# Block stack on one core: experts' front by token tile, norm factor moved, time mix with keys first

## What is computed

```
n   = rmsnorm(h, norm2_g)
q   = (n @ w_q) in 8 heads of 2 x 128
s1, s2 = q[:128] @ keys1.T, q[128:] @ keys2.T        (128 scores each)
16 best of s1, 16 best of s2, 16 best of their 256 sums -> idx (of 16384 experts), ts
g   = softmax(ts)
act = gelu(sum_d u[idx] * n)
out = sum_k (g * act)_k * v[idx]_k
```

## Time and profile before

| | us |
|---|---|
| runs shown (3) | 1532.51, 1533.3, 1535.24; median 1533.3 |
| the profiled execution, its own time | 1537.3 |
| its span in the trace | 1535.5 |
| PE, DVE, ACT, POOL busy | 1353.6, 819.4, 406.3, 293.1 |
| first gather issued | 866.96 |
| last dot begins | 1522.87 |
| mean granted clock of PE | 0.976 |

### The profile page before, as it was taken

How to read it: one execution, slowest core, us unless ns; L and a number is a source line. 1 busy time by engine, 2 the same in 40 slices (tenths; PEclk the granted TensorE clock), 3 DMA queues, 4 the chain that set the end, 5 groups by cost and what they waited for, 6 DMA issues and landing times. The chain is left out here.

```text
span 1535.5 us, 18607 instructions
## 1 busy us (share of the span) xinstructions
PE 1353.6 (88%) x7074; PEld 884.5 (58%) x7074; DVE 819.4 (53%) x1944; ACT 406.3 (26%) x955; POOL 293.1 (19%) x269
## 2 busy tenths in 40 slices
PE   5999999989999899999999799998777777777776
PEld 3445799978577786888888645443323333333322
DVE  6305567425633143422211767777777777777654
ACT  3003312111152115355101322222222232222212
POOL 0000000000000010000000244446443444444430
PEclk8999999999999999999999999999999999999999
DMA  7443100044322424532244599999999999999994
GB/s 264 137 151 127 53 3 3 1 156 132 124 91 87 139 76 136 173 110 83 89 154 150 211 421 421 421 421 423 420 421 422 420 422 421 421 422 421 421 421 197
DMA packets 65108, 367.97 MB, mean 240 GB/s; under 512 B 7229, under 2 KB 8637, under 8 KB 31933
## 3 DMA queue, kind: packets, MB, share of 16 engines
q0 software_dynamic: 37152, 269.50, 42.3%
q1 hardware_dynamic: 27870, 97.30, 18.7%
HBM read 365.72 MB, written 1.05 MB: 239 GB/s over the span
## 5 line engine op out<-in xcount | busy, mean ns | idle before, releaser
L2056 PE MATMUL bank<-arena 128*128 128x512 f32 x580 | 273.4, 616 | 75.0 <-ACT arena L2130 74.9
L1475 PE MATMUL bank<-arena,ring 128*128 128x256 f32 (+1 forms) x1136 | 254.9, 385 | 7.1 <-DVE arena L1738 3.1
L2282 POOL DMA_INDIRECT arena<-peer_in,arena x145 | 162.3, 1119 | 499.2 <-DVE arena L2199 311.9
L2056 PEld LDWEIGHTS bank<-arena 128*128 128x128 f32 x580 | 108.0, 194 | 232.3 <-issue 231.8
L1475 PEld LDWEIGHTS bank<-arena,ring 128*128 128x128 f32 x1136 | 215.6, 191 | 41.2 <-issue 3.5
L2249 DVE CUSTOM_DVE_ANT_0 arena<-arena 128x1024 f32<-128x1024 f32 x145 | 176.9, 1225 | 74.6 <-DMA arena<-peer_in,arena 74.4
L2130 ACT ACTIVATE arena<-cst,arena 128x128 f32<-128x128 f32 x256 | 88.8, 394 | 139.9 <-DVE arena L2212 139.9
L442 PE MATMUL bank<-ring,arena 128*128 128x512 f32 x256 | 112.5, 602 | 0.0
L2056 PE MATMUL bank<-ring,arena 128*128 128x512 f32 x176 | 86.5, 632 | 26.2 <-ACT arena L2130 26.2
L2123 ACT ACTIVATE arena<-arena 128x2 f32<-128x2 f32 x128 | 26.0, 203 | 304.1 <-DVE arena L2249 304.0
L442 PEld LDWEIGHTS bank<-ring,arena 128*128 128x128 f32 x256 | 49.4, 193 | 62.1 <-issue 62.1
(11 more groups left out here) (349 smaller groups left out, 1832.0 us busy)
## 6 DMA issues: line engine op xcount, KB each, us to landing
ring<-stream_in SPq DMA_DIRECT2D x162, 512.0 KB, 3.3
ring<-stream_in SPq DMA_DIRECT2D x8, 384.0 KB, 5.0
arena<-peer_in,arena POOLq DMA_INDIRECT x145, 34.5
row<-rows_in SPq DMA_DIRECT2D x4, 512.0 KB, 18.3
cst<-cst_in SPq DMA_DIRECT2D x1, 1929.0 KB, 18.1
res<-res_in SPq DMA_DIRECT2D x2, 544.0 KB, 4.3
row<-rows_in POOLq DMA_DIRECT2D x2, 512.0 KB, 4.8
cst<-rg_w_in SPq DMA_DIRECT2D x1, 1024.0 KB, 7.1
```

Of the source, the lines that this page charges most:

```text
L1475: mm = nc.tensor.matmul(bank[:, first:first + width], slot[:, at + k * cols:at + (k + 1) * cols], src[:, k, :], start=k == 0, stop=k == kt ...
L2056: mm = nc.tensor.matmul(core.banks[2 * t + b][:, :], diag[i % ND], value_half(i, b), start=first, stop=last)
L2282: pool.indirect_dma_start(out=places[seat[i]], out_offset=None, in_=g.names["peer"], in_offset=bass.IndirectOffsetOnAxis(ap=index[:, i:i + ...
```

## The change

1. **Time mix.** The stream has the key slots first and the LoRA slot behind them. DVE makes the mixture k first, then w, a, v, r, g. PE projects k first, waiting for two column blocks of the mixture at a slot, then does LoRA and z, then v, r, g. ACT copies the keys first.
2. **Mixing projection.** In the second mix PE does the eight panels for tile 0 alone (128 columns). DVE adds each to x and multiplies the sum by the norm's gain (`g.n2`, without the norm's factor). ACT's squares go. The ring keeps the eight slots; tile 1's panels (`mix_second`) are done in the experts' stage, four to a bank.
3. **First queries.** Queries 0 and 1 leave the ring: their weights come to a place of their own (`first_wq`), issued behind the last mixing slot. They are computed tile by tile.
4. **The norm's factor.** Ones-matmul, root, reciprocal and scaling in front of the queries go. Scores and dots are made from the unnormed n2. ACT's `root(t)` squares the turned x row by row with a sum, and takes the root; DVE inverts it to `rstd[:, t]` (one number for each token). The exponential takes `chosen - max` times it, the Gelu the dot times it.
5. **Order in the experts' stage.** On PE: first queries of tile 0, scores(0), turns of n2 and x for tile 0, `mix_second`, first queries of tile 1, turns of x and n2 for tile 1, queries 2 and 3, scores(1), then the pairs; queries 4 and 5 and scores(2) stand behind the first three pairs. DVE routes unit 0, adds tile 1's banks, scales n2's tile 1, and takes the first dots; it routes unit 1 in one piece behind the third pair, and unit 2 by five steps behind each pair from the fifth on.
6. **Places.** 9 at first; 3 (res, first_wq, the mixing input) when x of tile 1 has been turned; 5 from gather 72 on.

```diff
 def weight_slots():
-    out = [("lora", 2 * KT * LORA)]
+    out = []
     for name in ("k", "v", "r", "g"):
         out += [((name, half, kp), SLOT) for half in range(2) for kp in range(KT // 2)]
+        if name == "k":
+            out += [("lora", 2 * KT * LORA)]
...
-    out += [(("wq", m), SLOT) for m in range(2 * HP)]
+    out += [(("wq", m), SLOT) for m in range(FIRST, 2 * HP)]
...
@@ time mix, PE
+            def project(n, name):
+                if n:
+                    pe.wait_ge(mixed.handle, 3 * KT + n)
...
+                        if not n and not half:
+                            pe.wait_ge(mixed.handle, 2 * kp + 2)
...
+            project(0, "k")
             slot = core.weights(pe, "lora")
...
@@ time mix, DVE
-            for name, n in (("w", 1), ("a", 4), ("k", 2), ("v", 3), ("r", 0), ("g", 5)):
+            for name, n in (("k", 2), ("w", 1), ("a", 4), ("v", 3), ("r", 0), ("g", 5)):
...
@@ time mix, SP
-            core.load_weights(sp, g.stream, 1)
+            core.load_weights(sp, g.stream, RING)
             sp.dma_start(lora2[0:LORA + 1, :], g.low2_in).then_inc(*g.lora_loaded.dma())
-            core.load_weights(sp, g.stream, RING)
...
@@ second mix, PE
-                panel("mix", m, tiles(Y, T), KT, T).then_inc(*full(("mix", m)))
-                core.used_by(("mix", m), ("mix", m))
+                bank = claim(pe, ("mix", 0, m))
+                panel("mix", m, tiles(Y, T)[:, :, 0:P], KT, P, bank=bank).then_inc(*full(("mix", 0, m)))
...
@@ second mix, ACT
-            for m in range(KT):
-                copied(act, ("mix", m))
-                nc.scalar.activation(g.squares_d[:, m, :], x[:, m, :], ACT.Square).then_inc(*g.squared_d.up())
...
@@ second mix, DVE
-                nc.vector.tensor_tensor(x[:, m, :], x[:, m, :], bank[:, 0:T], ALU.add).then_inc(*free(key))
+                nc.vector.tensor_tensor(x[:, m, 0:P], x[:, m, 0:P], bank[:, 0:P], ALU.add).then_inc(*free(key))
+                copied(dve, key)
+                nc.vector.tensor_scalar(g.n2[:, m, 0:P], x[:, m, 0:P], vec("norm2", m), None, ALU.mult).then_inc(*g.gained.up())
...
@@ second mix, SP
-            core.load_weights(sp, g.stream, core.slot_no[("mix", KT - 1)] + 1 + RING)
+            core.load_weights(sp, g.stream, core.slot_no[("mix", KT - 1)] + 1)
+            at = P * sum(width for _, width in core.slots)
+            for m in range(FIRST):
+                src = g.stream[at + m * P * SLOT:at + (m + 1) * P * SLOT].rearrange("(p w) -> p w", p=P)
+                sp.dma_start(g.first_wq[:, m * SLOT:(m + 1) * SLOT], src).then_inc(*g.first_loaded.dma())
...
@@ experts, PE
-            pe.wait_ge(g.squared_d.handle, KT)
-            bank = take("ss_d")
-            for j in range(KT):
-                mm = nc.tensor.matmul(bank[:, 0:T], cst("ones"), g.squares_d[:, j, :], start=j == 0, stop=j == KT - 1)
-            mm.then_inc(*full("ss_d"))
+            def first_query(m, t):
...
+            def mix_second(quad):
...
+            pe.wait_ge(g.first_loaded.handle, 16 * FIRST)
+            first_query(0, 0)
+            first_query(1, 0)
             pe.wait_ge(keys_loaded.handle, 16)
-            query(0)
-            query(1)
             scores(0)
             turn("n2", n2, 0)
+            turn("x", x, 0)
+            mix_second(0)
+            mix_second(1)
+            first_query(0, 1)
+            first_query(1, 1)
+            turn("x", x, 1)
+            turn("n2", n2, 1)
             query(2)
             query(3)
             scores(1)
-            turn("n2", n2, 1)
-            query(4)
-            query(5)
-            scores(2)
-            turn("x", x, 0)
-            turn("x", x, 1)
...
+                    if n == 0 and q < 2:
+                        query(4 + q)
+                    if n == 0 and q == 2:
+                        scores(2)
...
@@ experts, ACT
+            def root(t):
+
+                copied(act, ("turn", "x", t, 1))
+                nc.scalar.activation(diag_flat, half(R, t), ACT.Square, accum_out=rstd[:, t:t + 1]).then_inc(*squared.up())
...
-                nc.scalar.activation(unit(weight, n), unit(chosen, n), ACT.Exp, bias=neg_max[:, n:n + 1],
+                act.wait_ge(scale_ready.handle, t + 1)
+                nc.scalar.activation(unit(weight, n), unit(weight, n), ACT.Exp, scale=rstd[:, t:t + 1],
...
@@ experts, DVE
-            for n in range(2):
-                for _ in route(n):
-                    pass
+            for _ in route(0):
+                pass
+            scale(0)
+            for quad in range(2):
+                key = ("mix", 1, quad)
+                bank = filled(dve, key)
+                at = x[:, 4 * quad:4 * quad + 4, P:T]
+                nc.vector.tensor_tensor(at, at, tiles(bank[:, :], P), ALU.add).then_inc(*free(key))
...
+            nc.vector.tensor_tensor(n2[:, :, P:T], x[:, :, P:T], gain, ALU.mult).then_inc(*g.gained.up())
...
-                    for _ in range(3):
+                    for _ in range(3 if n else 5 if q >= 4 else 0):
                         next(routing, None)
                     coefficients(n, q)
+                    if n == 0 and q == 2:
+                        for _ in route(1):
+                            pass
+                        scale(1)
```

More of the change, by code:

```diff
@@ L196, in pack_weights @@
     out = []
-    for key, width in weight_slots():
+    for key, width in weight_slots() + first_queries():
         if key == "lora":
@@ L2131, in _ @@
                           .then_inc(*diag_ready.up())
+                    if n == 0 and q in (1, 2):
+                        query(3 + q)
+                    if n == 0 and q == 3:
+                        scores(2)
+                    if n == 0 and q == 4:
+                        exps(1)
                     if asked:
```

173 lines of the change are left out of this document (106 added, 67 removed).

## The result

| | before | after |
|---|---|---|
| runs compared, median (lowest to highest), us | 1533.5 (1532.5 to 1535.2), 4 runs | 1519.7 (1516.5 to 1520.9), 4 runs |
| ratio, 95% interval | | 0.991 (0.989 to 0.992) |
| the profiled execution, us | 1537.3 | 1516.5 |
| span | 1535.5 | 1514.7 |
| mixing of the second mix begins | 812.07 | 807.64 |

The same kernel again, in a later comparison, gave 1516.85 (1515.5 to 1519.4, 4 runs), ratio 0.988 (0.986 to 0.990). All eight runs lie between 1515.5 and 1520.9; their median is 1517.8.

A forecast was written before the change was run, and what follows sets the result against it. A compute chain bounds the kernel up to the first gather, then a full DMA queue of 256 gathers. Terms -1.0 - 24.0 + 7.5 = -17.5 from 1537.3 give 1519.8, less 4.0 for the median 1515.8; range 1507 to 1525.

The forecast's parts named there:

- The lead: Way from the start of the second mix's mixing projection to the first gather: 24.0 us shorter.
- Bytes behind the first gather: DMA queue: ten 0.5 MB loads there instead of four, +7.5 us, bounds 0 and 8.
- The supply behind the first gather: Release of places to gathers in unit 0: later than before, but the queue never runs dry, so cost 0.
- the smallest: Smallest cover of the DMA queue: 7 us at gather 16, with 5 to 8 us for pairs 3 to 7.
- Time mix: Keys first in the time mix: PE's second wait goes and the clock may rise sooner, -1.0 us (0.35 to 1.65).
- a clock that rises 4.3 us: Time mix, upper bound: full clock at 24.8 instead of 27.4 us, worth 1.3 us more, 1.65 in all.
- The step from one execution to the median: Whole kernel: median of the runs taken as 4.0 us below the profiled execution, 1519.8 to 1515.8.
- passes paced by their weight loads: Rival for the 128-column matmuls: 160 passes each cost 0.078 us more, 12.6 us, total 1528; chance 2%.
- loads that cost nothing: Rival for the loads behind the first gather: they fall in idle DMA room, total 1508; chance 8%.
- half clock: Rival: clock stays at 0.50 through unit 0, eight pairs 38 us late, 31 after cover, total 1547; chance 4%.
- The broken supply: Rival at gather 16: unit 0's chain 7 to 14 us longer, queue dry up to 7 us, total 1523; chance 18%.
- the front gains nothing: Rival: the first gather does not bind the end, so no change, 1533; chance 3%.

The follow-up runs named there:

- norm_back: Changed kernel with the removed norm chain (ones-matmuls, ACT copy, DVE reciprocal) put back before the first queries, result unused: 1525.1 us, ratio 0.9941.
- keys_alone: Kernel before with only the time mix of the changed kernel (keys first): 1533.1 us, ratio 0.9988.
- tile1_first: Changed kernel with tile 1's mixing panels done before the first queries and their banks added before route(0): 1528.0 us, ratio 0.9956.
- front_alone: Changed kernel with the time mix of the kernel before: 1519.3 us, ratio 0.9894.
- less_weights: Changed kernel with queries 10 to 15 loading an eighth of their weight slots, so some experts differ from the reference: 1518.7 us, ratio 0.9895.
- late_four: Changed kernel with weights of queries 12 to 15 loaded before the first gather, into two places free only at gather 72: 1523.5 us, ratio 0.9924.
- early_less: Changed kernel with pairs started sooner in unit 0 and queries 10 to 15 loading an eighth of their slots: 1516.7 us, ratio 0.9885.
- full_again: The changed kernel run again without an edit: 1516.85 us, ratio 0.988.

## Why the prediction was right, point by point

**The total.** Forecast 1515.8, range 1507 to 1525; measured 1519.7 and 1516.9, 1517.8 over both. The sum against the profiled execution was -17.5; the profiled execution of the changed kernel came out 20.8 lower, and the medians 13.8 and 17.7 lower. The first gather, forecast at 841 to 843, left at 838.93 and 837.34, because more than the forecast had been gained before the mixing (see the time mix below). The other signs held: share 1.0 in unit 0, and a phase between 660 and 666.

**The lead, -24.0 forecast, -23.6 measured.** Its terms: mixing of tile 0 27.89 to 14.56 (-13.33; forecast -13.36), the norm gone from the path (norm_back gives 5.85 back of the 6.65; it puts back neither the first scaling nor ACT's full chain), queries 3.81 where 3.63 was forecast. Half the width took little more than half the time: 128 passes of 128 columns took 14.56, 14.46 and 14.53 us in three places (tile 0, tile 1, and the earlier trace rows), 0.114 each, where a 256-column pass took 0.218.

**Bytes behind the first gather, +7.5 forecast, phase +7.1 to +8.3 measured** (my upper bound was 8). Ten loads were forecast and counted. The phase goes with their number: four, 655.9 and 655.3 us (before, keys_alone); six, 659.3 (tile1_first); ten, 663.0 to 664.2 (the changed kernel twice, front_alone 663.8). From four to ten that is 1.2 to 1.5 us a load, against 1.25. This holds for kernels whose queue stays full; less_weights, late_four and early_less are the others.

**The supply behind the first gather, at nothing: right, with a cover mis-sized.** In us after the first gather: first Gelu 23.7 (forecast 23.5), route(1) from 35.5 (32.4), gather 16 at 46.2 (43). The 3 us are the low clock from 862.7 to 869.5, which halves PE in that stretch; full_again, with 3.4 us of it, had gather 16 at 43.7. The cover there was 4.8 and 7.3 us, where I had said 7. What failed is "the smallest": near gather 30 it is 3.4 to 5.8, where I had said 5 to 8. The step behind it is the pace of the pairs: I put 5.3 us in unit 0 and 4.6 from unit 1 on, against 5.0 of DMA. Between gathers 16 and 30 seven pairs took 38.9 and 39.0 us in the two profiles, 5.6 each, while 14 gathers and two loads are 37.5, or 5.4 each. I had also put ACT's Gelus at nothing, as the same instructions; with their scale they took 295 ns instead of 203, and they stand between a pair's dots and its release. The kernel kept a rest of cover, so the time came out right. But what a reader would have taken from the first part of the prediction, that a byte less behind the first gather gives its time back, holds in one direction only: four loads more cost theirs (tile1_first against the changed kernel), six loads less gave nothing.

**Time mix, -1.0 forecast.** keys_alone gives -1.8 (-3.4 to -0.5), the timeline -0.88 at 120 us. That is from one pair of profiles: over all of them this place was reached at 118.69 to 120.50 with keys first, and at 120.82 and 121.88 with the time mix of before. The 1.65 us of half clock behind it, which went with the time mix in every profile, were not in my sum, so the -1.0 may be too small. PE did not wait again after its first matmul:

```profile
20.32 30.73 PE L434 MATMUL bank<-ring,arena 128*128 128x512 f32 x64 [8.79 <-DVE arena L830]
50.98 7.12 PE L450 MATMUL bank<-arena,ring 128*64 128x256 f32 x32
```

and LoRA was wanted at 51, not 49. The table load in front of the tanh took 1.28 us from 51.70, and the tanh then waited until 54.69 for the first LoRA product, so the load was hidden, as forecast. What did not hold in this profile is my upper bound, a clock that rises 4.3 us after PE's first matmul: it was 0.50 from 16.2 to 26.4, so it rose 6.1 us after that matmul. The low stretch was as long as before (17.3 to 27.5) and ended 1.1 us sooner. In keys_alone it ended at 23.9, 3.1 us after the first matmul (20.76).

**The step from one execution to the median, -4.0.** I took the difference of the kernel before and used it for the one after. It is not a property of the kernel: the profiled execution of before lay above its four runs, that of the changed kernel was the lowest of its four, 3.2 us below their median. Against the profiled execution my sum was 3.3 us short (1519.8 for 1516.5); against the two medians, 1519.7 and 1516.9, the forecast of 1515.8 is 3.9 and 1.1 low, and without the step it would be 0.1 and 2.9 high. Which of them fits best within these 4 us is luck. Of the 4.43 us before the mixing 1.70 are of this kind.

The rivals: passes paced by their weight loads are ruled out by 14.56 (114 ns a pass, with weight loads of 191 ns in L1494's mean), loads that cost nothing by the phase. A half clock came in unit 0 (862.7 to 869.5) and cost nothing, since the queue had work (share 1.02, 421 GB/s in that stretch). The broken supply did not come in this kernel; less_weights and late_four show what it looks like. That the front gains nothing is ruled out by front_alone.

## What to carry to other kernels

Split a kernel like this at the first transfer of its bound queue: what lies ahead is a chain and is worth every microsecond (5.85 us put back cost 7.3 here), what lies behind is a sum of bytes, and a thing moved across the border pays its bytes (1.2 to 1.5 us for each load of 0.5 MB here). Before counting on fewer bytes, follow the supply of buffers at every release and not only at the first late one: cover is work queued less time passed, its smallest place can be one or two units further on, and with less in the queue it shrinks by just what was saved. And before giving a few microseconds to a change or to chance, compare the same stretch of code in all profiles at hand: two executions put 3.35 us down to chance here, and thirteen showed that only half of it changed from one execution to the next.

## What the runs showed of the hardware

- A matmul of f32 stands in the trace as two records: tile 0's mixing has 64 in the program and x128 at L1494, the one-column ones are 16 and x32 at L478. A record of 256 columns took 0.218 us, one of 128 columns 0.114 (27.89 and 14.56 by 128).
- The granted clock was 1.00 or 0.50: of 891 slices of 1.7 us before, 834 had 1.00, 27 had 0.50, and the other 30 stand at the edges of low stretches. It fell to 0.50 for 3.4, 6.8 or 10.2 us (but for stretches that the end of the profile cuts off), and in front_alone once for 13.7, also where the profile shows PE busy throughout (129.9 to 136.7 before). Some of these stretches differ between executions of one kernel (at 130.8 for 3.4 us and not at all there in two profiles of the changed one). Where PE sets the pace each costs half its length: 41.25, 39.60 and 37.90 us for the same work with 6.8, 3.4 and none. Behind the first gather it came out of the cover: 862.7 to 869.5 at 0.50, with the DMA share at 1.02.
- In the changed kernel SP's 0.5 MB loads landed in 8.1 to 8.7 us (before: 7.7 to 9.6) while a dozen gathers of 1 MB stood in POOL's queue, against 3.3 for all loads of the kernel in the median; a gather took 33 to 35 us to land (median for each of its buffers, in the profiles before and after). So the loads did not wait for the gathers that were issued before them.
- A Gelu of 128x2 with a scale for each partition took 295 ns in the median (the changed kernel), without it 203 (before; 128 of each). No run tries what that costs.
